# Two transformer stacks in one kernel: attention values weighed turned, and side work placed ahead of the weight split

## What is computed

```
for i in range(4):                       # first stack
    q, k, v, qm (and for A: qi, wi, ki) = split(x @ w_in[i]);  rope(q), rope(k)
    mix = attention over 12 heads of 64  # A: only the 64 best keys of an indexer score (top-k)
                                         # B: 4 heads x 3 dilations, joined by log-sum-exp, values 192 wide
                                         # C: causal
    mo = attention of qm over 256 memory rows, 4 heads (keys, values = mem_n @ w_mem_kv[i])
    x = layer_norm(ALPHA * x + concat(mix, mo) @ w_out[i])
    x = layer_norm(ALPHA * x + (silu(g) * u) @ w_down[i])      # g, u = x @ w_gate_up[i], 2816 wide
for i in range(2):                       # second stack
    h = rms_norm(x) * (1 + scale) + shift              # scale, shift, gate from c @ w_ada
    rq, rk, rv, rg, sq, sk, sv, sg = split(h @ w_in_2[i])
    y = concat(retention(rotary(rq), rotary(rk), rv) * silu(rg),
               stick_breaking(sq, sk, sv) * silu(sg)) @ w_out_2[i]
    x = x + gate * y
return rms_norm(x)
```

## Time and profile before

| | us |
|---|---|
| median of 3 runs | 1695.37 |
| lowest, highest | 1690.32, 1695.37 |
| the profiled execution | 1693.71 |
| its span, first to last instruction | 1691.9 |
| TensorE busy in it | 1613.1 |
| mean granted TensorE clock | 0.982 of full speed |

### The profile page before, as it was taken

How to read it: one execution, slowest core, us unless ns; L and a number is a source line. 1 busy time by engine, 2 the same in 40 slices (tenths; PEclk the granted TensorE clock), 3 DMA queues, 4 the chain that set the end, 5 groups by cost and what they waited for, 6 DMA issues and landing times. The chain is left out here.

```text
span 1691.9 us, 20176 instructions
## 1 busy us (share of the span) xinstructions
PE 1613.1 (95%) x8388; PEld 1337.0 (79%) x8388; DVE 1061.3 (63%) x1439; ACT 721.5 (43%) x862; POOL 52.8 (3%) x89
## 2 busy tenths in 40 slices
PE   6899999999999999999999999999999989999998
PEld 5898788888777878878788888787888868787876
DVE  5575667566566765575667656857676575557635
ACT  4435444433443433445443443454433434444352
POOL 2000000000000000000000000000100010000000
PEclk9799999999999999999999999999999989999999
DMA  8552257654523766352466744413756435334420
GB/s 262 190 203 100 101 205 271 231 215 161 196 98 139 274 222 250 129 220 76 145 240 225 262 165 170 156 74 129 278 224 260 173 148 197 125 122 148 167 111 25
DMA packets 45035, 299.89 MB, mean 177 GB/s; under 512 B 5444, under 2 KB 5700, under 8 KB 11280
## 3 DMA queue, kind: packets, MB, share of 16 engines
q1 hardware_dynamic: 38736, 278.48, 44.9%
q0 software_dynamic: 5776, 19.01, 3.6%
q10 hardware_dynamic: 432, 1.11, 0.2%
HBM read 296.20 MB, written 2.65 MB: 177 GB/s over the span
## 5 line engine op out<-in xcount | busy, mean ns | idle before, releaser
L824 PE MATMUL psum<-w_high,xt_high 128*128 128x512 f32 (+1 forms) x1472 | 581.0, 395 | 20.8 <-DVE xt_low L1339 12.7
L1145 ACT ACTIVATE w_high<-w_raw 128x2048 fp32r<-128x2048 f32 x241 | 458.8, 1905 | 287.9 <-DMA w_raw<-in_weights 176.2
L1313 DVE TENSOR_TENSOR w_low<-w_raw,w_high 128x2048 fp32r<-128x2048 f32 x241 | 546.7, 2272 | 53.0 <-ACT w_high L1145 52.3
L826 PE MATMUL psum<-w_high,xt_low 128*128 128x512 f32 (+1 forms) x1472 | 568.9, 387 | 0.0
L825 PE MATMUL psum<-w_low,xt_high 128*128 128x512 f32 (+1 forms) x1472 | 568.0, 386 | 0.0
L824 PEld LDWEIGHTS psum<-w_high,xt_high 128*128 128x128 f32 x1472 | 281.1, 191 | 88.9 <-issue 12.3
L826 PEld LDWEIGHTS psum<-w_high,xt_low 128*128 128x128 f32 x1472 | 280.4, 191 | 56.7
L825 PEld LDWEIGHTS psum<-w_low,xt_high 128*128 128x128 f32 x1472 | 281.4, 191 | 51.5
L1606 DVE TENSOR_TENSOR arena<-arena,psum 128x256 f32<-128x256 f32 x88 | 37.0, 420 | 215.9 <-ACT arena L1236 215.5
L824 PE MATMUL psum<-w_high,ht_high 128*128 128x512 f32 x352 | 141.5, 402 | 0.0
L826 PE MATMUL psum<-w_high,ht_low 128*128 128x512 f32 x352 | 138.2, 393 | 0.0
(11 more groups left out here) (221 smaller groups left out, 1642.5 us busy)
## 6 DMA issues: line engine op xcount, KB each, us to landing
w_raw<-in_weights SPq DMA_DIRECT2D x263, 1024.0 KB, 4.8
norm_params<-in_ln_g POOLq DMA_DIRECT2D x8, 512.0 KB, 4.1
norm_params<-in_ln_b POOLq DMA_DIRECT2D x8, 512.0 KB, 5.7
kv_outside<-arena POOLq DMA_DIRECT2D x3, 512.0 KB, 2.9
mem_kv<-kv_outside POOLq DMA_DIRECT2D x3, 512.0 KB, 3.5
norm_params<-mods_outside POOLq DMA_DIRECT2D x3, 512.0 KB, 6.4
x_rows<-in_x SPq DMA_DIRECT2D x2, 512.0 KB, 8.8
w_raw<-in_weights SPq DMA_DIRECT2D x2, 512.0 KB, 6.2
```

Source lines behind the costliest of these rows:

```text
L824: e.matmul(dst, a_hi, b_hi, start=first, stop=False)
L826: return e.matmul(dst, a_lo, b_hi, start=False, stop=last)
L1145: e.activation(K.w_hi[:, g % RING, 0:w], K.w_raw[:, r, 0:w], ACT.Copy).then_inc(K.high.hit(t), 1)
L1313: e.tensor_tensor(K.w_lo[:, s, 0:w], K.w_raw[:, r, 0:w], K.w_hi[:, s, 0:w].bitcast(F32), ALU.subtract).then_inc(K.taken.hit(t), 1)
```

## The change

- `weigh` exchanges its operands: values (64 columns) are stationary, the turned probabilities (128 columns) stream, and a head's result lands turned, in one half of the partitions of the bank. Heads of even number go to partitions 0 to 63, of odd number to 64 to 127; a 192 wide value of kind B is three strips. ScalarE copies the bank to `mixed_t`. `xt` for the output product has no transposes left; high and low parts are made from `mixed_t`, for each half as soon as its units are done (`first_turned`, `first_rows`, `last_rows`).
- The reciprocal is multiplied into the probabilities by VectorE in `recip`, before they are turned.
- `on` does side work first and `split` behind it. Rotations (`keys_turned`, `queries`, `rotations`) are begun at the product that makes their input, not one later; `late` in `block`, the second residual in `second`, and rms and modulate of row block 0 among the last down products are placed ahead of a split.
- `group` and `first_columns` take one more block of which they do the first half tile for each row block, in the `wide` ring; its second half follows. This is done in layer 3 of the first stack and in both layers of the second.
- The indexer keys are turned one step after its queries, `rotated` has a step more, the first stick-breaking scores are made two steps earlier, memory rows are turned behind the narrow products, and layer 0's block 0 of row block 1 is evacuated by VectorE.

```diff
         for g in groups:
-            use = self.xt_uses[gen, rb, g] = self.tr.take()
-            after = self.units[gen[1], rb][g - 2] if gen[0] == "mix" else None
...
 
+        self.step_background()
         self.split()
-        self.step_background()
+
+    def ahead(self):
+
+        if self.owed:
+            self.owed -= 1
+            self.high()
 
...
-                    late()
                 self.gemm(t, rb, half, gen, "gemm", uses[rb])
                 if half:
                     then(rb, uses[rb], t)
+                if late and not rb and not half:
+                    late()
                 self.on()
...
                     after[rb][len(blocks) * half + n]()
+            if more:
+                uses_more.append(self.wide.take())
+                self.gemm(t_more, rb, 0, gen, "wide", uses_more[rb], prompt=prompt)
+                after[rb][-1]()
+        if more:
+            self.second_half(more, gen, uses_more)
+
...
+                    elif layer == 1:
+                        self.xt(("mem",), n, (1,))
...
+        yield
...
+                elif step == FF_STEPS - 1:
+                    if layer == LAST:
+                        self.next_rows(layer, 0)
+                elif layer == LAST:
+                    self.last_downs(step)
                 else:
...
                     self.split()
...
+                self.split()
             self.norm(out, rb)
-            if layer == LAST:
-                self.add("rms", (0, rb))
-                self.add("modulate", (0, rb))
+        if layer == LAST:
+            self.add("rms", (0, 1))
+            self.add("modulate", (0, 1))
...
+    def last_downs(self, step):
+
+        if step == FF_STEPS - 3:
+            self.low()
+            self.add("rms", (0, 0))
+            self.ahead()
+            self.add("modulate", (0, 0))
+        else:
+            self.ahead()
...
+                else:
+                    self.beside(self.indexer_work(layer))
+                self.on()
+                self.gemm(t_more, rb, 0, gen, "wide", uses_more[rb], prompt=True)
+                self.on()
+            self.second_half(more, gen, uses_more)
         if layer == 0:
             self.beside(self.early_work())
             self.block(w_in, at, 3 * MIX, gen, qi[-1], late=lambda: self.xt(gen, 1))
             project(0)
-            narrow([self.split] * 2)
...
-            self.on()
-            self.beside(self.turn_heads(layer, "k", 0))
-
-        def second_keys():
-            self.on()
-            self.beside(self.turn_heads(layer, "k", 1))
-        self.group([keys], gen, [[self.on, first_keys], [self.on, second_keys]], True)
+        def keys_turned(rb):
+            def then():
+                self.beside(self.turn_heads(layer, "k", rb))
+                self.on()
+            return then
+        self.group([keys], gen, [[self.on, keys_turned(0)], [self.on, keys_turned(1)]], True)
...
+            self.xt(mix, 0, (0,))
+            self.on()
+
         def turned():
             if kind == "B":
                 self.on()
                 self.step_background()
             assert len(self.units[layer, 0]) == len(own[0]) + 1
-            self.xt(mix, 0)
+            self.xt(mix, 0, (1,))
             if kind != "B":
                 self.on()
...
+        def units_on():
+            self.on()
+            if KINDS[layer] == "B":
+                self.step_background()
+
+        def first_rows():
+            self.xt(mix, 1, (0,))
+            self.on()
+
+        def last_rows():
             self.on()
             self.drain()
...
         def second():
+            self.add("residual", late[1])
             self.split()
-            self.add("residual", late[1])
             self.norm(key, 1)
         self.group([("w_out", layer, h * BLK, "half", sums(h)) for h in range(2)], mix,
-                   [[self.on, self.on, self.on, rest], [self.split, self.split, turned, second]], True)
+                   [[units_on, first_rows, last_rows, rest], [self.split, self.split, turned, second]], True)
...
+        yield
...
 
+        pairs = [self.stick_breaking(layer, n) for n in range(SB_H // 2)]
+        next(pairs[0])
         yield
         yield
-        yield from self.pipelined([self.stick_breaking(layer, n) for n in range(SB_H // 2)])
+        yield from self.pipelined([self.begun(pairs[0]), *pairs[1:]])
+
...
-        def keys():
+        def rotations(rb):
+            def then():
+                if rb == 0 and layer == 0:
+                    self.add("load_decay")
+                if rb:
+                    self.drain()
+                self.beside(self.rotated(layer, rb))
+                self.on()
+                if rb:
+                    if layer + 1 < DEPTH_2:
+                        self.add("load_modulation", layer + 1)
+                    self.add("load_gate", layer)
+            return then
+
+        def rows():
+            late()
             self.on()
-            self.beside(self.rotated(layer, 1))
-        self.group([proj(0), proj(1)], gen, [[self.split, self.split, late, queries], [self.on] * 3 + [keys]])
-        if layer + 1 < DEPTH_2:
-            self.add("load_modulation", layer + 1)
-        self.add("load_gate", layer)
-        project(2)
+        self.group([proj(0), proj(1)], gen, [[self.split] * 3 + [rotations(0), rows], [self.on] * 3 + [rotations(1), self.on]],
+                   layer == 0, proj(2))
         self.drain()
...
-        elif stage == "mix":
-            pe.wait_ge(*K.tr.out(j.after.out))
-            src = K.mixed[:, rb, :]
...
-            if j.kind == "dil":
-                pe.wait_ge(*K.joined.at(j.n))
-            else:
-                pe.wait_ge(*K.wide.out(j.wide))
+            pe.wait_ge(*K.shared_out.at(j.n))
...
             pe.wait_ge(*K.tr.out(use))
-        for n, h in enumerate(j.heads):
+        work = strips(j)
+        for s, _ in work:
+            if j.kind != "mem":
+                for kb in range(nk // P):
+                    if s < (4 * BLK - 2 * MIX) // HD:
+                        pe.wait_ge(*K.made(("proj", j.layer, 3), kb))
+                    else:
+                        pe.wait_ge(*K.made(("tail", j.layer), 0))
+        first = work[0][0] // 2
+        for chunk in range(first, work[-1][0] // 2 + 1):
             for kb in range(nk // P):
-                if j.kind == "mem":
-                    c0, w, rows = MEMW + h * HD, HD, K.kv
-                else:
-                    w, rows = DIL_V if j.kind == "dil" else HD, K.proj
-                    c0 = 2 * MIX + h * w
-                    if c0 < 4 * BLK:
-                        pe.wait_ge(*K.gemms.out(plan.blocks[("proj", j.layer, 3), kb]))
-                    if c0 + w > 4 * BLK:
-                        pe.wait_ge(*K.gemms.out(plan.blocks[("tail", j.layer), 0]))
-                c = n * (nk // P) + kb
-                m = e.matmul(psum[:, to, n * w:n * w + w], K.probt[slot][:, c * P:c * P + P], rows[:, kb, c0:c0 + w],
-                             start=kb == 0, stop=kb == nk // P - 1)
+                for s, n in work:
+                    if s // 2 == chunk:
+                        rows, c0 = (K.kv, MEMW + (s - NH) * HD) if j.kind == "mem" else (K.proj, 2 * MIX + s * HD)
+                        c, p0 = n * (nk // P) + kb, HD * (s % 2)
+                        m = e.matmul(psum[p0:p0 + HD, to, (chunk - first) * P:(chunk - first) * P + P], rows[:, kb, c0:c0 + HD],
+                                     K.probt[slot][:, c * P:c * P + P], start=kb == 0, stop=kb == nk // P - 1)
...
-        act.wait_ge(*K.turned.at(j.use))
-        e.activation(hi[:, 4 * j.g:4 * j.g + 4, j.rb * P:j.rb * P + P],
-                     psum[:, K.tr.place(j.use), :].rearrange("p (c s) -> p c s", s=P),
-                     ACT.Copy).then_inc(K.xt_high.hit(j.use), 1)
+        act.wait_ge(*(K.tr.out(j.after.out) if j.after else K.turned.at(j.use)))
+        e.activation(hi[:, 4 * j.g:4 * j.g + 4, j.rb * P:j.rb * P + P], K.left_from(j),
+                     ACT.Copy).then_inc(K.xt_high.hit(j[:3]), 1)
 
...
+    def weigh(j):
+
+        work = strips(j)
+        first, last = work[0][0], work[-1][0]
+        act.wait_ge(*K.turned.at(j.out))
+        a, z = (first + 1) // 2, (last + 1) // 2
+        to, bank = K.mixed_t[j.rb], psum[:, K.tr.place(j.out), :].rearrange("p (c s) -> p c s", s=P)
+        if first % 2:
+            e.activation(to[HD:P, first // 2, :], bank[HD:P, 0, :], ACT.Copy)
+        if last % 2 == 0:
+            e.activation(to[0:HD, last // 2, :], bank[0:HD, last // 2 - first // 2, :], ACT.Copy)
+        e.activation(to[:, a:z, :], bank[:, a - first // 2:z - first // 2, :], ACT.Copy).then_inc(K.tr.sem(j.out), 1)
+
...
     def recip(j):
+
         nk, slot = unit_keys(j), j.prob % 2
         n = 1 if j.kind == "dil" else len(j.heads)
+        pr = K.prob[slot][:, 0:n * nk]
         v.wait_ge(*K.wide.out(j.wide))
-        if j.prob >= 2 and plan.prob_user[j.prob - 2][0] == "unit":
```

(20 more changed lines are left out.)

140 lines of the change are left out of this document (84 added, 56 removed).

## The result

The kernel after takes 1700.31 us (median of seven runs, 1698.77 to 1704.48), the kernel before 1694.87 us (1690.32 to 1695.37) on the same chip: ratio 1.0045, 95% interval 1.0029 to 1.0061. The forecast was 1671, and faster; the change made the kernel slower by 5 us, 0.3%, little but clear of the interval.

The account below looks back on a forecast made before the run. TensorE, busy 1613.1 of 1691.9 us, was taken as the bound. Terms of -50.2 and +27.5 gave net -22.7 us from the profiled 1693.7, so 1671.0 us; 8-in-10 range 1650 to 1690.

Parts of the forecast that it names:

- -8.6 + 2: Turned values on TensorE: 64 transposes of `mixed` removed, -8.6 us; weighing matmuls with new switches between forms, +2 us.
- clock, counted apart: Opening and clock: low-clock stretches behind the removed TensorE waits were to go, -6 of 30 us not granted.
- The 7.8 us for xt_low: TensorE's waits for xt_low before output products and layer 3's first columns, and in the opening: 7.8 of 12.7 us go.
- The copy moves to ScalarE, behind the exponentials: Attention steps: second transposes wait for a bank that ScalarE empties after four exponentials; 6.1 us a layer, +18.3 in three.
- rival (d): Slower: waits of 1.4 to 1.9 us lower the clock in attention stretches; 1696 to 1722 us, chance 0.08.
- the normalisation: VectorE multiplies probabilities before their transposes: +3.6 us in layers' second steps, +3.6 for delaying the maximum.
- Side work in front of the split: Rotations, kept products, indexer keys and `x_rows` no longer wait behind a low half on VectorE: -19.1 us.
- the later low half: Low half and w_raw release move back by at most some 3 us, against a five-tile ring never shown empty: 0.
- rival (c): Waits return at the next instruction and low halves become late; half the gain, 17 us, lost: 1688 us, chance 0.10.
- Rival (b): Weighing matmuls on column halves do not overlap, so the upper price holds: +13, 1684 us, chance 0.12.
- rival (a): ScalarE's copy does not hold TensorE, as exponentials finish before the weighing; the 18.3 us go: 1652.7 us, chance 0.20.

## Why the prediction was wrong

Run by run, the way from before to after can be walked in four steps, each a difference of two medians, beside the terms of my sum:

| step | my terms | measured |
|---|---|---|
| side work first (before to side work alone) | -19.1 | -28.7 |
| all else but the turned values (to the old weighing in the new plan) | -7.8 - 4.7 - 4 = -16.5 | -8.5 |
| turned values, copy on VectorE | -8.6 + 2 + 3.6 + 3.6 = +0.6 | +7.0 |
| the copy to ScalarE behind the exponentials | +18.3 | +35.8 |
| clock, counted apart | -6 | in the rows above |
| sum | -22.7 | +5.6 |

The 7.8 us for xt_low stand in the second row because of the waits: 12.4 us with side work alone, 3.3 with the old weighing in the new plan, and 3.3 again with the values turned. I had put them down to the removed transposes; what removes them is the plan, which makes the low halves earlier.

The steps do not quite add whatever their order (side work first is worth 28.7, 30.2 or 35.2 us by what stands around it), but the size of the error, 28.3 us, is far above that.

**The step that failed is "The copy moves to ScalarE, behind the exponentials": right in mechanism, mis-sized, 18.3 us for 35.8.** The list of waits was foreseen (one new line, about 15 times, 20 to 30 us; it is 16 times, 35.6 us). The 34.2 us between the two profiled spans divide into 21.3 of idle time, near my 18.3, and 12.9 of busy time, the clock. So the larger part of the error is the clock. I set rival (d) apart, at 0.08, as if a wait under 2 us in a step of 8 to 9 could not bring it, and counted -6 us of clock for all. Its range, 1696 to 1722, holds the result; its chance was too low because I treated it as another mechanism, while it is what this same wait does next. That the range holds the result is luck in part: the rival took at least 25 us for the clock, 12.9 were measured, and the rest is made up by the two steps below. The smaller part is a step that I had priced at nothing, as VectorE was late in it already: it has the longest wait of all, 2.78 us where the kernel before waits 1.51.

```profile
1158.62 1.23 DVE L1677 TENSOR_TENSOR work<-work,recip 128x1024 f32<-128x1024 f32 x1
...
1159.77 1.22 DVE L1660 TENSOR_REDUCE neg_max<-psum 128x4 f32<-128x1024 f32 x1
...
1162.89 0.39 ACT L1328 ACTIVATE arena<-psum 128x256 f32<-128x256 f32 x1
1163.34 0.48 PE L1099 MATMUL psum<-ident,work 128*128 128x128 f32 x1 [2.78 <-ACT arena L1328]
```

The scores end at 1158.78, but the maximum starts at 1159.77, behind the multiplication, and passes its lateness on to exponentials and copy.

**The second wrong step is the normalisation**: +3.6 for the second step of a layer and +3.6 for delaying the maximum, 7.2 in all. It is 19.0 us with the copy on VectorE and 9.6 with the copy on ScalarE. I counted it only where its transposes follow their exponentials directly and where a low half of `mixed` stands in the same step; it is also in front of the maximum in the others, and the clock takes its share. Without the multiplication the turned values are worth 1645.5 - 1657.5 = -12.0 us, for my -8.6 + 2 = -6.6: the sums took 30.9 us for 47.2, where I had 37.9 and let those 9 us count for nothing.

**Side work in front of the split** was under-priced by 9.6 us. Idle time fell by 19.2 us, which meets my 19.1 by luck, as it is in part at other places: `x_rows` stayed, the weights of values (7.9 to 2.8) I had not counted. The clock behind the waits, 6.9 us, was in another term.

**The third wrong step is the later low half, which I put at 0**, since no row showed an empty ring of tiles. With the 7.8 us in their place, "all else" was to give 16.5 us and gave 8.5. The waits that it was about did go: xt_low 12.4 to 3.3, the modulated rows 7.0 to 0.7, `x_rows` 2.2 to nothing. What came for them are low halves, with the old weighing as well: of weights 1.1 to 14.1 us, of memory rows 2.1 to 4.5, together 15.4. The line of xt_low with side work alone, then three lines of the old weighing in the new plan:

```profile
PE psum L824 <- DVE xt_low L1339: 12.4, 7, 4.6
```

```profile
PE psum L903 <- DVE w_low L1399: 14.1, 8, 6.7
...
PE psum L903 <- DVE memt_low L1425: 4.5, 2, 2.6
PE psum L903 <- DVE xt_low L1425: 3.3, 4, 1.1
```

The ring did not run empty; the low half stood in VectorE's own order behind rows that wait for other engines, 6.67 us at one place in the kernel after, and in its opening 2.63 and 2.66 us. That is rival (c)'s mechanism, in about its size, and it would have shown in the order of the plan: what follows `split` at the start of the second stack. In part it is made up by the last layer's down products and layer 3's columns, whose stages are 5.2 and 6.5 us shorter after than before; why the first are is not shown.

**Rival (b)** is out by the weighing's 30.9 us, and **rival (a)** by the 35.6 us of waits. The Trainium skill (TensorEngine Tiling (Array Packing), PSUM Bottleneck) says that tiling speeds TensorE but not the way out of PSUM, and that both engines should copy. The trace agrees with the first half: the tiled sums are faster by 16.3 us (47.2 to 30.9) and the kernel is not. The second half did not decide here: with both engines emptying the transposes' banks in all runs, the copy of the sums on VectorE (1664.5 us) was better than on ScalarE behind its exponentials (1700.3), and on ScalarE ahead of them it was near that (1670.1).

## What to carry to other kernels

When an eviction moves to another engine, read what stands in front of it in that engine's order, not how busy the engine is: 0.5 us of copy behind 1.9 us of exponentials that wait for a maximum cost 35.8 us with 16 waits, and changing the order of the step gave back 30.2. Price a new wait on TensorE with the clock that the rows show behind such waits (here 12.9 us, on top of some 21 of idle time), and price a lateness through the whole chain, also in steps that look late already. An edit of a few lines whose gain can be read off the waits (side work ahead of the split, -28.7 us) is worth running alone before it goes in with others that hide it.

## What the runs showed of the hardware

- Matmuls with 64 columns of weights on alternate halves of the columns take 74 ns a record for 128 streamed columns (30.9 us for 416), where 187 ns was the row for a whole array and 91 ns the one for alternate halves of the rows.
- Of 15 waits of 2.0 to 2.8 us on TensorE for the copy (layers 0, 2 and 3 of the kernel after), 12 had the 1.2 GHz level behind them: 7 matmuls of 512 columns in 2 us. The kernel before has it once behind 1.68 us. With waits of 0.4 us at the same place the granted clock of 20 us was 1.00 (copy on VectorE, the first window), and in the same run a wait of 2.14 us, for the multiplication, which ends at 1143.87, has 0.50 behind it (the second):

```profile
1106.00:1126.00 20.00, 18.00 (x141) 13.80 (x138) 12.50 (x16) 10.70 (x31) 0.00 (x0) 1.00 0.00 1
...
1146.00:1148.00 2.00, 2.00 (x6) 1.54 (x5) 1.45 (x1) 0.00 (x0) 0.00 (x0) 0.50 0.00 0
```

- The copy out of PSUM costs about the same on both: 0.55 us on VectorE and 0.50 us on ScalarE for 384 columns.
